# A chunked recurrence's triangular inverse on one core: the transposed matrices by 128x128 transposes in place of 64x64 products

## The reference, cut to what matters

```python
def wkv7_scan(r, w, k, v, kk, a, reverse):
    def step(state, inp):
        r_t, w_t, k_t, v_t, kk_t, a_t = inp
        sa = jnp.einsum('bhij,bhj->bhi', state, -kk_t)
        state = (state * w_t[:, :, None, :] + sa[..., None] * (kk_t * a_t)[:, :, None, :]
                 + v_t[..., None] * k_t[:, :, None, :])
        return state, jnp.einsum('bhij,bhj->bhi', state, r_t)
```

## Time and profile before

| | |
|---|---|
| median of three runs | 3892.47 us (3888.59 to 3895.09) |
| span of the profiled execution | 3891.5 us |
| TensorE busy, weight loads | 3726.6 us (96%), 2991.8 us (77%) |
| VectorE, ScalarE, GpSimd busy | 1682.0, 1439.6, 1385.9 us |
| the chain that ended last | TensorE 84%, of it line 1127 10% |
| two recurrences | about 120 to 366 us and 1240 to 1486 us of the span |
| one group in the middle of a recurrence | 28.3 to 31.6 us |

### The profile page before, as it was taken

The page is one execution under the profiler, slowest core; times in us unless marked ns, Lnnn a source line. Parts: engine busy times, 40 slices in busy tenths (PEclk is TensorE's granted clock), DMA queues, the critical chain, the costliest instruction groups (busy, mean ns, idle before and its releaser), DMA issues.

```text
span 3891.5 us, 67184 instructions
## 1 busy us (share of the span) xinstructions
PE 3726.6 (96%) x28976; PEld 2991.8 (77%) x28976; DVE 1682.0 (43%) x2714; ACT 1439.6 (37%) x2450; POOL 1385.9 (36%) x581
## 2 busy tenths in 40 slices
PE   8888999999999889999999999999999999999999
PEld 7777768888887776688888876578888776688887
DVE  6554441477245554612683158515111376332112
ACT  3454252323323442523223243634222436433222
POOL 5001324444443002144444454234444453244443
PEclk9999999999999999999999999999999999999999
DMA  3001212266221001122473222112322221122222
GB/s 146 2 4 46 84 67 96 87 248 235 87 87 44 4 4 66 70 112 87 162 269 142 87 98 76 44 68 100 108 87 90 105 87 65 45 87 87 87 108 87
DMA packets 37151, 356.66 MB, mean 92 GB/s; under 512 B 4224, under 2 KB 4352, under 8 KB 17920
## 3 DMA queue, kind: packets, MB, share of 16 engines
q1 hardware_dynamic: 19584, 278.93, 19.4%
q10 hardware_dynamic: 17280, 73.48, 5.3%
HBM read 350.29 MB, written 2.10 MB: 91 GB/s over the span
## 4 chain that ended last, share of the span: by engine, by line
PE 84%; DVE 7%; ACT 4%; issue 2%; DMA 1%; PEld 1%; POOL 0%; PEldq 0%; DVEq 0%; SPq 0%; ACTq 0%; POOLq 0%
PE banks L768 23%; PE banks L770 23%; PE banks L769 23%; PE banks L1127 10%; PE banks L2179 3%; ACT arena L2335 2%; ACT arena L1495 2%; PE banks L2261 1%; DMA ring<-stream 1%; DVE arena L1975 1%; DVE arena L1869 1%; PE banks L1249 0%; DVE x L2736 0%; PE banks L1447 0%; DVE arena L1986 0%
## 5 line engine op out<-in xcount | busy, mean ns | idle before, releaser
L866 POOL TENSOR_TENSOR ring_r<-ring,hi_ring 128x1024 fp32r<-128x1024 f32 x490 | 1204.4, 2463 | 2176.6 <-ACT hi_ring L857 2176.2
L768 PE MATMUL banks<-xT_r,ring_r 128*128 128x512 f32 (+1 forms) x2480 | 951.9, 384 | 11.9 <-issue 7.9
L770 PE MATMUL banks<-xT_r,hi_ring 128*128 128x512 f32 x2096 | 826.5, 394 | 0.0
L769 PE MATMUL banks<-x_lo_r,hi_ring 128*128 128x512 f32 x2096 | 823.3, 393 | 0.0
L857 ACT ACTIVATE hi_ring<-ring 128x1024 fp32r<-128x1024 f32 x490 | 511.2, 1047 | 719.6 <-DMA ring<-stream 302.3
L768 PEld LDWEIGHTS banks<-xT_r,ring_r 128*128 128x128 f32 x2480 | 470.3, 190 | 108.5 <-issue 15.8
L770 PEld LDWEIGHTS banks<-xT_r,hi_ring 128*128 128x128 f32 x2096 | 394.2, 188 | 92.6
L769 PEld LDWEIGHTS banks<-x_lo_r,hi_ring 128*128 128x128 f32 x2096 | 396.4, 189 | 89.2 <-issue 3.3
L1127 PE MATMUL banks<-arena 64*64 64x64 f32 (+4 forms) x7456 | 341.9, 249 | 53.4 <-DVE arena L1869 22.8
L1495 ACT ACTIVATE arena<-banks 128x512 f32<-128x512 f32 x366 | 214.6, 595 | 402.0 <-PE banks L770 242.9
L770 PE MATMUL banks<-hi_ring,pairs 128*128 128x512 f32 x864 | 342.5, 396 | 0.0
(11 more groups left out here) (262 smaller groups left out, 5393.0 us busy)
## 6 DMA issues: line engine op xcount, KB each, us to landing
ring<-stream SPq DMA_DIRECT2D x132, 2048.0 KB, 7.7
arena<-ada ACTq DMA_DIRECT2D x96, 512.0 KB, 5.1
arena<-ln_rows ACTq DMA_DIRECT2D x5, 1024.0 KB, 7.8
arena<-edge ACTq DMA_DIRECT2D x4, 1024.0 KB, 5.0
arena<-edge ACTq DMA_DIRECT2D x2, 1792.0 KB, 7.6
arena<-pack ACTq DMA_DIRECT2D x2, 1485.0 KB, 6.9
arena<-pack ACTq DMA_DIRECT2D x2, 1200.5 KB, 5.5
x<-x_in SPq DMA_DIRECT2D x4, 512.0 KB, 7.5
```

The lines of the kernel that those rows point to most:

```text
L768: first = nc.tensor.matmul(out_, left[1], right[0], start=start, stop=False)
L769: low = nc.tensor.matmul(out_, left[0], right[1], start=False, stop=False)
L770: return first, low, nc.tensor.matmul(out_, left[0], right[0], start=False, stop=stop)
L866: nc.gpsimd.tensor_tensor(feed.raw(n, ring_r), feed.raw(n), feed.hi(n).bitcast(F32), ALU.subtract).then_inc(split_lo, 1)
```

## The change

- At levels 0 to 3 the products inv_t are gone. A new step inv_r(n-1) stands beside inv_a(n), behind it: four 128x128 transposes of X (two 64x64 blocks side by side make one 128x128 block each) into bank 6, which ScalarE copies to XT. inv_t stays at level 4 alone, as a product.
- A transposed pair of blocks lands in XT with p and e exchanged, so from level 1 on inv_a, inv_x and inv_t take and leave their blocks in a matching order: within each q the four products go through the quadrants alternating between the row halves, and each row half always writes to the same bank.
- inv_x(n+1) waits for inv_r's copy where it waited for inv_t's.
- r0 stands beside inv_x(1) in place of inv_a(4).

```diff
@@ -168,9 +168,8 @@
            [("x0", g, (b0,)), ("turned", g, 1, (b1,))], [("turned", g, 2, (6,))]]
     for n in range(len(LEVELS)):
         last = n == len(LEVELS) - 1
-        banks_a, banks_x, banks_t = (b0,), (b0,) if n else (6,), (b0,) if n == 0 or last else (6,)
-        out += [[("inv_a", g, n, banks_a)] + ([("r0", g, (6,))] if last else []),
-                ([] if last else [("inv_x", g, n, banks_x)]) + [("inv_t", g, n, banks_t)]]
+        out += [[("inv_a", g, n, (b0,))] + ([("inv_r", g, n - 1, (6,))] if n else []),
+                ([("inv_t", g, n, (b0,))] if last else [("inv_x", g, n, (b0,) if n else (6,))]) + ([("r0", g, (6,))] if n == 1 else [])]
     out += [[("wu", g, (b0, b1))], [("mq", g, (b0, b1))], [("oo", g, ())]]
     out += [[("link", g, i, (4 + i % 2,) if i < NC - 1 else ())] for i in range(NC)]
     if g == GROUPS - 1:
@@ -1117,7 +1116,7 @@
 
     def wide(name, level):
 
-        return name == "inv_t" and level in (0, len(LEVELS) - 1) or name in ("inv_a", "inv_x") and level > 0
+        return name in ("inv_a", "inv_x", "inv_t") and level > 0
 
     def first_tensor(pe, k_, layer, uses):
         feed = feed1[layer]
@@ -1261,24 +1260,37 @@
                 elif name != "inv_a":
                     drained(pe, uses, "inv_a", g, args[1])
                     if args[1]:
-                        drained(pe, uses, "inv_t", g, args[1] - 1)
+                        drained(pe, uses, "inv_r", g, args[1] - 1)
                 elif args[1]:
                     drained(pe, uses, "inv_x", g, args[1] - 1)
                 else:
                     drained(pe, uses, "x0", g)
                 level = args[1] if len(args) > 1 else 0
                 for q in range(4):
-                    for e in range(2):
-                        for p_ in range(2):
-                            n, straight, crossed = 2 * q + e, side(p_), side(p_ ^ e)
-                            h = crossed if level and name in ("inv_x", "inv_t") else straight
-                            to = crossed if name == "inv_a" and level or name == "inv_t" and level < len(LEVELS) - 1 else straight
-                            left, right = {"x0": (XT[d][h, n, :], C("ident2")[h]), "r0": (GM[d][h, q, e, 1, 0, :], V[g // 2 % 2][h, q, e, :]),
-                                           "inv_a": (GM[d][h, q, e, 0, 0, :], X[d][h, n, :]), "inv_x": (XT[d][h, n, :], T1[d][h, n, :]),
-                                           "inv_t": (T1[d][h, n, :], XT[d][h, n, :])}[name]
-                            at = (4 * e + q if wide(name, level) else n) * CH
-                            to = across(banks[0])[to, at:at + CH] if wide(name, level) else bank[banks[0]][to, at:at + CH]
-                            ins = mm(to, left, right, True, True)
+                    for k, p_ in HALVES if wide(name, level) else ():
+                        if name == "inv_a":
+                            e = p_ ^ k
+                            left, right, to, at = GM[d][side(p_), q, e, 0, 0, :], X[d][side(p_), 2 * q + e, :], side(e), 4 * p_ + q
+                        else:
+                            p_, e = p_ ^ k, p_
+                            turned_, t1 = XT[d][side(e), 2 * q + p_, :], T1[d][side(e), 2 * q + p_, :]
+                            left, right = (turned_, t1) if name == "inv_x" else (t1, turned_)
+                            to, at = side(p_), 4 * e + q
+                        ins = mm(across(banks[0])[to, at * CH:(at + 1) * CH], left, right, True, True)
+                    for e, p_ in () if wide(name, level) else HALVES:
+                        h, n = side(p_), 2 * q + e
+                        left, right = {"x0": (XT[d][h, n, :], C("ident2")[h]), "r0": (GM[d][h, q, e, 1, 0, :], V[g // 2 % 2][h, q, e, :]),
+                                       "inv_a": (GM[d][h, q, e, 0, 0, :], X[d][h, n, :]), "inv_x": (XT[d][h, n, :], T1[d][h, n, :])}[name]
+                        ins = mm(bank[banks[0]][h, n * CH:(n + 1) * CH], left, right, True, True)
+                ins.then_inc(bank_full[banks[0]], 1)
+            elif name == "inv_r":
+
+                g, level = args
+                take(banks[0], use[0])
+                drained(pe, uses, "inv_x", g, level)
+                for q in range(4):
+                    ins = nc.tensor.transpose(bank[banks[0]][:, q * P:(q + 1) * P],
+                                              X[g % 2][:, 2 * q:2 * q + 2, :].rearrange("p e t -> p (e t)"), C("ident"))
                 ins.then_inc(bank_full[banks[0]], 1)
             elif name == "wu":
                 g, d = args[0], args[0] % 2
@@ -1569,9 +1581,9 @@
                 filled(b, n)
                 f((XT if name == "inv_t" else X)[args[0] % 2].rearrange("p (q e) t -> p e q t", e=2),
                   across(b).rearrange("p (e q t) -> p e q t", e=2, q=4), ACT.Copy).then_inc(bank_free[b], 1)
-            elif name in ("x0", "inv_x", "inv_t"):
+            elif name in ("x0", "inv_x", "inv_r"):
                 filled(b, n)
-                f((XT if name == "inv_t" else X)[args[0] % 2], bank[b][:, :].rearrange("p (b t) -> p b t", b=8), ACT.Copy)\
+                f((XT if name == "inv_r" else X)[args[0] % 2], bank[b][:, :].rearrange("p (b t) -> p b t", b=8), ACT.Copy)\
                     .then_inc(bank_free[b], 1)
             elif name == "r0":
                 filled(b, n)
```

## The result

The changed kernel takes 3907.71 us as the median of five runs (3902.94 to 3910.61), beside 3892.82 (3888.59 to 3895.09) of the kernel before in the same session: ratio 1.0037, 95% interval 1.0026 to 1.0048. It is slower by 15 us, more than the 0.2% that can be told from no change, and outside the predicted range.

A forecast was written before the change was run, and what follows sets the result against it. The prediction took the inverse, a latency loop over TensorE, VectorE and ScalarE, as the bound; loop 11 us longer and instruction relief 8 us shorter made 3 us longer, 3895 us, range 3883 to 3905.

The forecast's parts named there:

- TensorE's own sum: Per group, 3.26 us of inv_t go and 2.80 of inv_r come; TensorE alone would win 7 us over 16 groups.
- The rule on the drain: Changing the tiling mode drains TensorE; inv_r would start 0.07 us later, at most 3 us more in all.
- Level 0 to 1: inv_a(1) starts 0.46 us earlier, but inv_x(1) then waits for inv_r(0)'s copy; gain kept 0.04 us.
- Level 1 to 2, "nothing": r0 (0.95 us) replaces inv_t(1) (0.92) beside the copy of X; without r0 nothing would come sooner.
- Level 2 to 3, the loss: On ScalarE, exponentials queue behind inv_r(1)'s copy and X's copy behind them: 0.64 us lost in odd, 1.14 in even cases.
- Level 3 to 4: The next group's Gram product waits for VectorE, so removing inv_t(3) gains nothing; 0.04 us taken off for inv_a(3)'s spread.
- The sum of the loop: The level-by-level changes in both layers' recurrences add up to 5.6 us a layer, 11 us longer for two.
- The instructions: TensorE stops for late instruction fetches, 12 us in the recurrences; 3584 fewer records relieve two thirds, 8 us shorter.
- the third rival: The granted clock falls in the thinner levels, 1 us a group for 14 groups: 3909 us; chance 0.05.
- Rival 1: Instructions to TensorE were the real bound, many small stops included; 20 us won gives 3883 us; chance 0.19.
- Rival 2: ScalarE's queue costs 11 us and fetches still come late, or copies slip further: 3903 to 3906 us; chance 0.20.
- Rival 4: The new product order makes wide sets take 0.92 us instead of 0.69 on TensorE: 3910 us; chance 0.04.

The follow-up runs named there:

- r0 elsewhere: The changed kernel with r0 behind inv_x(2), or behind inv_x(3), instead of behind inv_x(1): 3897.65 us and 3899.32 us.
- VectorE's copy: The changed kernel with the copy of inv_r(1) to XT on VectorE instead of ScalarE: 3890.82 us, ratio 0.9999 to the kernel before.
- the kernel before with r0 moved: The kernel before with r0 alone moved from inv_a(4) to behind inv_x(1) and inv_t(1): 3911.53 us, ratio 1.0056.
- the wide filling: The changed kernel with one unread 128x128 by 384-column product added behind inv_x(2) and inv_x(3): 3906.21 us, ratio 1.0037 to the kernel before.
- the small filling: The changed kernel with 16 unread 64x64 products added behind inv_x(2) and behind inv_x(3): 3901.89 us, ratio 1.0024 to the kernel before.

## Why the prediction was wrong

By its own steps, with the distances between the first products of inv_a(n) in us, odd and even group behind where they differ:

| step | before | predicted | after |
|---|---|---|---|
| level 0 to 1 | 4.80 | 4.34 | 4.41 |
| level 1 to 2 | 3.35 | 3.77 | 3.85 |
| level 2 to 3 | 3.92 / 3.42 | 4.56 | 4.60 / 4.58 |
| level 3 to 4 | 4.95 / 5.01 | 4.91 / 4.97 | 4.95 / 4.95, at full clock |

**TensorE's own sum** held: inv_r takes 0.66 us and starts 0.07 before the modelled end of inv_a (256.83 against 256.21 + 0.69). The rule on the drain, Trainium skill, TensorEngine Tiling (Array Packing), Key Properties, would have had it start at the end; here too the row is 0.07 us shorter than the rule.

**Level 0 to 1** was right in kind: inv_a(1) comes 0.39 us sooner, not 0.46, and inv_x(1) waits for ScalarE's copy instead of the mask (258.27, idle put down to ScalarE). But the hand-over takes 0.14 to 0.15 us where I had 0.06: from the end of the copy (257.53 + 0.60 = 258.13) to 258.27. That turns "0.04 kept" into a small loss.

**Level 1 to 2, "nothing"** failed, and so did its reason. The step said that without r0 nothing would come sooner. Both kernels with r0 elsewhere show 3.55 instead of 3.85. r0 ends so late that the link and inv_a(2) start behind it, not behind the copy of X (259.02 + 0.60 = 259.62; inv_a(2) starts at 260.15). Levels 0 to 2 together take 8.26 us, before 8.15.

**Level 2 to 3, the loss** is what it was said to be, mechanism and size: 4.58 to 4.60 for 4.56, a loss of 0.68 and 1.16 for 0.64 and 1.14. The experiment with VectorE's copy takes it away.

**Level 3 to 4** was right where the clock is full.

**The sum of the loop** came out at 9.8 us for groups 1 to 6 (2 x 4.9) and measures 12.1. The 2.3 that are missing are 12 groups of some 0.19: 0.15 of levels 0 to 2 (0.11 lost where I had 0.04 gained), the rest from level 2 to 3 and from the 0.04 at level 3 to 4, which came with one parity only.

**The instructions** were near in size, not shown in kind: 8 us of relief forecast; 6.4 of stops before in groups 1 to 6, none in the first profile after and one of 1.8 in the second, a relief of 5.5. That the stops are missing instructions, and that thinner levels end them, stays unproven: the kernel before with r0 moved loses them without losing a record, and the stop of 1.8 stands at level 2, one of the thinned ones.

**The step that failed** is the clock, which the forecast left out. It was the third rival, with a chance of 0.05 and a price of 1 us a group for 14 groups, 3909 us in all; measured are 3907.7, falls in 8 of the 12 groups and about 1 us for each. The price of a fall was right, the chance far too low. That its 3909 comes so near is in part luck: it charged 14 groups, and the loop and the smaller relief filled what the groups without a fall left. Taken out, the clock's 7.4 us leave about 3900, an estimate from the bookkeeping, inside the range, which the fillings' times don't confirm. The earlier trace rows had shown a fall: granted clock 0.74 over levels 0 to 3 of group 0, which has no links. The prediction's own timetable said that level 2 becomes thin too: behind inv_x(2) nothing but a link until the copy of X, and behind inv_x(3), where inv_t(3) is gone, nothing until gram. Two idles of over a microsecond, one level apart, are what distinguishes the new group from the old one. I took the row for a case of group 0, not for a price that other groups pay once they are as thin. The 0.05 came from no row. The row itself was weak evidence, as the second profile of before shows no fall at that place, while the changed kernel falls there every time. Whether transposes count as busy for the clock (Trainium skill, TensorE: Matmul & The Clock Gate, Part 4: they don't) no run here separates; with the wide filling the transposes stand as before and the clock doesn't fall in groups 1 to 6, so they don't bring it down by themselves.

The forecast net was +3: loop +11 and stops -8. Measured, in groups 1 to 6: loop +12, stops -5.5 and clock +7.4.

**Rival 1** (instructions the real bound) fell: the stops did go, there was no more in it than they, and the waits of the weight loads on which it rested grew. **Rival 2** (no relief) gave a time near the measured one, 3903 to 3906, for a wrong reason. **Rival 4** fell: wide sets still take 0.69 us in the new order. It rested on a misreading, which stands in the description of the kernel before, too: inv_t at levels 1 to 3 doesn't write from four quadrants to one bank. Its inputs and its outputs are crossed together (`h` and `to` in the old code), so it uses two quadrants like x0 and r0, and the 0.92 us that it adds are near r0's 0.95. What four quadrants into one bank would cost was not tried.

## What to carry over

A copy that is added to an engine in order is charged to everything behind it: list what the queue holds there, for each parity of the loop, and put the copy on the engine where it stands ahead of nothing. Moving a step needs the same look at its bank, not only at its engine. Work taken out of a loop that doesn't wait for it can cost twice, once by the wait that replaces it and once by TensorE's clock: where a trace of before shows a fall in the thinnest stretch, profile it again, and charge every stretch that becomes as thin with what the fall costs, times how often it comes.

## What the runs showed of the hardware

- The granted clock falls inside a loop in which TensorE's longest idles are 1.2 us: 0.57 to 0.58 over 4 us, at level 3 or from the end of it into level 4, in 8 of 12 groups, in both profiles. Groups with the same two idles kept 1.00 (group 5). At 1.2 GHz four 128x128 transposes took 1.12 us (0.66 at 2.4), a wide set of 16 products 0.99 and 1.05 (0.69).
- With one 128x128 product of 384 columns behind each of the two idle places no group of 1 to 6 fell, with r0 in one of them 5 and 3 did, and with the waits themselves shortened (VectorE's copy) 2, or 0 with r0 at level 2 or 3 besides.
- TensorE stops in the middle of sets without a wait of the program: 9.6 us in 12 places over two recurrences of 245 us before, 0.5 in 2 with r0 moved and no record fewer, 5.9 in 11 with the small filling in groups 1 to 6. Their cause isn't shown.
